# Other places, in the merged instruction order, for the three strands that run beside the cached pages

## The reference, cut to what matters

```python
# 1. the new tokens attend to the cached pages (64 pages of 128 tokens for each of 8 sequences)
kp = k_pool[page_table]; vp = v_pool[page_table]
s = concat([q @ kp, q @ k_new + mask]) ; w = softmax(s[0]) - lam * softmax(s[1]) ; o_b = w @ [vp, v_new]
# 2. gated delta rule over the prompt, 6 heads of 64: blocks with a triangular solve, then
v_new = u - w @ S ; o = q @ S + qk @ v_new ; S = S * g + k.T @ v_new
# 3. RWKV-7 over the prompt, 6 heads of 64, of the same shape, with its own decays, group norm and gate
# 4. keys and values of the prompt's memory (256 rows)
m = rmsnorm(mem, g) ; mk = m @ wk ; mv = m @ wv
```

## Time and profile before

| | |
|---|---|
| time, median of 3 runs | 5814.06 us (5811.03 to 5820.93) |
| the profiled execution | 5813.6 us, its span 5811.9 us |
| mean granted TensorE clock | 0.926 of full speed |
| busy, share of the span | PE 90%, PEld 56%, DVE 40%, ACT 26%, POOL 12% |
| the stage with the pages | from about 1351 to 2078 us of the span |
| that stage's PE | 555.3 us busy between 1353 and 2080 us |

### The profile page before, as it was taken

How to read it: one execution, slowest core, us unless ns; L and a number is a source line. 1 busy time by engine, 2 the same in 40 slices (tenths; PEclk the granted TensorE clock), 3 DMA queues, 4 the chain that set the end, 5 groups by cost and what they waited for, 6 DMA issues and landing times.

```text
span 5811.9 us, 91907 instructions
## 1 busy us (share of the span) xinstructions
PE 5255.0 (90%) x35274; PEld 3277.1 (56%) x35274; DVE 2329.3 (40%) x5433; ACT 1498.6 (26%) x3423; POOL 717.5 (12%) x935
## 2 busy tenths in 40 slices
PE   8989899996788667899989999999999899988998
PEld 5644445554556455666656555565555655656454
DVE  1156665553445423453434433343433534221322
ACT  3234543332222201221222221222212222112112
POOL 0012221111323201100101101011001110000000
PEclk9989999998989767799998999999999899997999
DMA  3110111104878523022231222312223122241232
GB/s 99 48 31 31 33 34 35 35 31 147 246 229 252 147 40 94 25 84 74 83 88 46 78 76 84 98 46 80 76 84 105 35 84 75 73 135 55 81 89 72
DMA packets 747337, 487.66 MB, mean 84 GB/s; under 512 B 78191, under 2 KB 728431, under 8 KB 746868
## 3 DMA queue, kind: packets, MB, share of 16 engines
q1 hardware_dynamic: 674134, 384.95, 23.2%
q10 hardware_dynamic: 60480, 63.27, 3.4%
q0 software_dynamic: 12288, 33.57, 1.9%
HBM read 432.57 MB, written 49.09 MB: 83 GB/s over the span
## 4 chain that ended last, share of the span: by engine, by line
PE 54%; DVE 4%; ACT 1%; issue 1%; DMA 1%; POOL 1%; SPq 0%; DVEq 0%; ACTq 0%; POOLq 0%
PE s_f_b L3493 27%; PE s_f_b L3551 11%; PE s_f_b L3542 2%; PE s_bank L2523 2%; PE s_bank L2530 2%; PE s_bank L2529 1%; DVE s_r_o L2795 1%; PE s_f_b L3532 1%; PE s_f_b L3498 1%; PE s_f_b L3514 0%; PE s_bank L2711 0%; PE s_bank L2666 0%; PE s_bank L3873 0%; PE s_bank L2708 0%; PE s_bank L3104 0%
## 5 line engine op out<-in xcount | busy, mean ns | idle before, releaser
L3493 PE MATMUL s_f_b<-s_f_h,s_f_W 128*128 128x416 f32 (+2 forms) x4480 | 1648.5, 523 | 26.3 <-DMA s_f_h<-o_t 17.1
L3493 PEld LDWEIGHTS s_f_b<-s_f_h,s_f_W 128*128 128x128 f32 x4480 | 845.2, 193 | 704.8 <-issue 585.8
L3551 PE MATMUL s_f_b<-s_f_a,s_f_W 128*128 128x416 f32 (+2 forms) x1760 | 640.0, 520 | 0.1
L539 PE MATMUL s_p_acc<-s_hT,s_p_W 128*128 128x416 f32 x1600 | 625.4, 538 | 6.8 <-DMA s_p_W<-in_w_in_dram 6.8
L3551 PEld LDWEIGHTS s_f_b<-s_f_a,s_f_W 128*128 128x128 f32 x1760 | 330.8, 191 | 266.2 <-issue 221.4
L539 PEld LDWEIGHTS s_p_acc<-s_hT,s_p_W 128*128 128x128 f32 x1600 | 299.4, 196 | 285.8 <-issue 269.3
L3751 DVE TENSOR_TENSOR s_f_xT<-s_f_xT,s_f_b 128x416 f32<-128x416 f32 (+2 forms) x160 | 93.7, 587 | 596.3 <-PE s_f_b L3551 531.4
L928 ACT ACTIVATE s_prob<-s_s_ps,s_ntop 128x512 f32<-128x512 f32 (+3 forms) x320 | 196.7, 620 | 369.1 <-DVE s_ntop L979 368.9
L3772 POOL TENSOR_TENSOR s_f_ex<-s_f_ex,s_f_mix 128x416 f32<-128x416 f32 (+2 forms) x105 | 112.2, 1069 | 1363.5 <-ACT s_f_mix L3580 1363.0
L3623 ACT ACTIVATE s_f_raw<-s_f_b 128x416 f32<-128x416 f32 (+2 forms) x110 | 56.9, 518 | 771.5 <-PE s_f_b L3493 771.5
L976 DVE TENSOR_REDUCE s_ntop<-s_s_ps 128x2 f32<-128x1024 f32 (+3 forms) x160 | 169.9, 1062 | 64.2 <-PE s_s_ps L876 61.7
(11 more groups left out here) (787 smaller groups left out, 7905.9 us busy)
## 6 DMA issues: line engine op xcount, KB each, us to landing
s_f_W<-in_ffn_w_in_dram SPq DMA_DIRECT2D x220, 512.0 KB, 3.8
s_K<-in_cache_diff_k_dram SPq DMA_DIRECT2D x384, 128.0 KB, 3.3
s_f_W<-in_ffn_w_out_dram SPq DMA_DIRECT2D x80, 448.0 KB, 3.8
s_V<-in_cache_diff_v_dram POOLq DMA_DIRECT2D x256, 128.0 KB, 3.8
s_V<-in_cache_diff_v_dram ACTq DMA_DIRECT2D x192, 128.0 KB, 3.7
cols_t<-s_p_out ACTq DMA_DIRECT2D x100, 208.0 KB, 1.9
s_f_W<-in_w_out_dram SPq DMA_DIRECT2D x40, 512.0 KB, 4.6
s_f_W<-in_ffn_w_out_dram SPq DMA_DIRECT2D x40, 512.0 KB, 4.1
```

The costliest lines, as they stand in the source:

```text
L539: mm = pe.matmul(self.acc[n % 2][:, 0:CH], self.W[:, u, k, :], self.hT[:, k, c * CH:(c + 1) * CH], start=(k == 0), stop=(k == KD - 1))
L3493: mm = pe.matmul(bank(u)[:, 0:G], w[:, k, :], h[:, k, 0:G], start=(k == 0), stop=(k == KD - 1 and kind != "op"))
L3551: mm = pe.matmul(bank(u)[:, 0:G], w[:, k, :], a[:, f % NA, 0:G], start=(k == 0), stop=(k == len(part) - 1))
```

## The change

`weave` gives way to `merge`, which takes an explicit list of places. The pages and the small loads keep theirs. The three strands beside the pages get new ones: D_ is spread evenly over 0 to 0.35, R_ over 0.37 to 0.72, W_'s first six slots stand at 0.735, 0.74, 0.775, 0.78, 0.785 and 0.79, and its `kv` slots at 0.81 to 0.89 in steps of 0.01. (`merge` stood in the kernel already, for a later stage.)

```diff
-                    n_slots = D_.slots + R_.slots + W_.slots
                     last = ((R_.stored, 16 * LEAD),)
+                    even = lambda lane: [(n + 0.5) / lane.slots for n in range(lane.slots)]
+                    stretch = lambda lane, a, b: [a + (b - a) * at for at in even(lane)]
+                    turn_at = stretch(D_, 0.0, 0.35) + stretch(R_, 0.37, 0.72) + [0.735, 0.74, 0.775, 0.78, 0.785, 0.79] + [0.81 + 0.01 * n for n in range(W_.slots - 6)]
                     turns = lambda eng, one, two, three: (
-                        in_turn(eng, in_turn(eng, one(eng), done, two(eng)), last, three(eng)), n_slots)
+                        in_turn(eng, in_turn(eng, one(eng), done, two(eng)), last, three(eng)), turn_at)
...
-                            weave((K_.sp(sp), K_.slots), turns(sp, D_.sp, R_.sp, W_.sp), (states(sp), len(loads)))
+                            merge((K_.sp(sp), even(K_)), turns(sp, D_.sp, R_.sp, W_.sp),
+                                  (states(sp), [(n + 0.5) / len(loads) for n in range(len(loads))]))
...
-                            weave((K_.pe(pe), K_.slots), turns(pe, D_.pe, R_.pe, W_.pe))
+                            merge((K_.pe(pe), even(K_)), turns(pe, D_.pe, R_.pe, W_.pe))
```

More of the change, by code:

```diff
@@ L4237, in _ @@
                             act.preload_act_table_set("natural_log_exp_and_others")
-                            weave((K_.act(act), K_.slots), turns(act, D_.act, R_.act, W_.act))
+                            merge((K_.act(act), even(K_)), turns(act, D_.act, R_.act, W_.act))
                         @block.vector
                         def _(dve):
-                            weave((K_.dve(dve), K_.slots), turns(dve, D_.dve, R_.dve, W_.dve))
+                            merge((K_.dve(dve), even(K_)), turns(dve, D_.dve, R_.dve, W_.dve))
                         @block.gpsimd
                         def _(pool):
-                            weave((K_.pool(pool), K_.slots), turns(pool, D_.pool, R_.pool, W_.pool))
+                            merge((K_.pool(pool), even(K_)), turns(pool, D_.pool, R_.pool, W_.pool))
                 levels = ss.sb("levels", [P, 7, P])
```

## The result

| | before | after |
|---|---|---|
| median | 5816.55 us (5 runs, 5811.03 to 5820.93) | 5844.84 us (5 runs, 5841.38 to 5847.66) |
| profiled span | 5811.9 us | 5846.0 us |
| granted clock, whole span | 0.926 | 0.924 |
| last store of the stage | 2076.11 us | 2111.64 us |

The ratio is 1.0049, with an interval of 1.0038 to 1.0059: the kernel became slower by half a per cent. The forecast was 5816 in a range of 5786 to 5843, so it missed on the slow side, where the chain rival stood (5838 to 5850). The stage's last store comes 35.5 us later and the span is 34.1 us longer, so all of the difference was made in this one stage.

The account below looks back on a forecast made before the run. PE was taken as the bound, near nine tenths busy nearly everywhere. K128 at 1949.1 - 14 + 26 + 4 + 43 + 7 + 7 - 9 + 3 = 2016, plus 63, gave 2079 for 2076.1, so 5816 us (5786 to 5843).

Parts of the forecast that it names:

- chain rival: Stage with cached pages: the recurrences' chain bounds, not PE; step 3 is 65 to 77 us, 5838 to 5850; chance 0.18.
- step 3: Ahead of K128, 32 pairs of strand slots without a page slot between: +43 us priced by hops, bounds 12 and 77.
- step 7: Ahead of K128, lower granted clock behind each of the new 7.5 us waits: +3 us.
- step 2: R_'s work and `tp` moved ahead of K128: +26 us of PE work, +4 of ordinary small waits.
- faster rival: Same stage: the pairs' hops vanish in waits the pages have anyway; 5786 to 5796 us; chance 0.28.
- post back: These slots side by side five times in D_ and R_: 18 us, the R_ tiles waiting 7.5 us each.
- mid flip: These slots side by side, among seven other pairs of step 3 at about 1 us each, 7 together.
- step 6: Waits for `E` and for the store at the change from D_ to R_ get hidden: -9 us (0 to -15).
- step 1: Stage's start: D_'s first load ahead of the pages brings K7 at 1398 for 1407: -14 us (9 to 19.5).
- steps 4 and 5: W_'s norm takes ACT from the pages, +7 us (2 to 12); lone page slots wait for V pages, +7 (0 to 15).
- DMA rival: V pages can't keep up in K115 to K127: 20 us and not 7, 5829; chance 0.10.
- Tail: From K128 to the stage's last store: 63 us, for 127 before.

Follow-up runs that it names:

- e5: The change with D_ spread evenly over 0 to 0.395, R_ over 0.395 to 0.80, and W_ later; ratio 0.9977 against the kernel before (-13 us).
- e10: The change with seven slots (back of D_1, D_2 and all R_ tiles, flip of R_1, R_2) put behind the next page slot; 1.0017 against the kernel before.
- e11: The change with D_ to 0.385, R_'s first slot at 0.387, its others evenly 0.395 to 0.803, W_ later; 0.9958 against the kernel before.
- e1: The kernel before with only D_'s first slot put ahead of the pages' first; ratio 1.0001 against the kernel before (+1 us).
- e12: e11 with the lane of small loads (constants and old states) starting at 0.1 of the order, not 0; ratio 0.9964 against the kernel before.
- e2: The change with W_ put back to its old places behind the pages; ratio 1.0088 against the kernel before (+51 us).
- e7: The change with D_ still dense (0 to 0.35), R_ widened to 0.37 to 0.80, W_ as in e5; ratio 1.0004 against the kernel before.
- e9: The change with D_ over 0 to 0.44, R_ still dense (0.45 to 0.80), W_ as in e5; ratio 1.0014 against the kernel before.

## Why the prediction was wrong, step by step

**The steps that failed are step 3, in the choice between its two bounds, and step 7, the clock.** Step 3 priced the pairs by the hop between two slots that stood uncovered at the end of R_ (43 us in all) and set aside "if the chain bound everywhere" (77). Step 7 gave the slower matmuls 3 us. The two traces say how far each was off. Up to the transposes of K127 (columns as in rows 2, before and after):

```profile
1351.00:1949.10 598.10, 461.96 (x5579) 328.58 (x5579) 281.75 (x600) 161.48 (x304) 171.68 (x277) 0.86 0.75 226
1351.00:2050.80 699.80, 513.15 (x6126) 370.68 (x6127) 301.65 (x641) 171.80 (x326) 178.63 (x288) 0.83 0.66 199
```

| up to K127, us | forecast | measured |
|---|---|---|
| start and key pages | -14 | -9 |
| waits of the recurrences (`s_shared`) | +47 (steps 2 and 3) | +76 |
| the pages' other waits | +5 (steps 4 to 6) | -17 |
| PE busy | +29 (26 of step 2, 3 of step 7) | +51 |
| in all | +67 | +102 (the parts, rounded, 101) |

The three rows of waits are sums over PE's list of waits, and the first has the idle time from 1351 us to PE's first product too. So the recurrences waited as the chain rival had it. The faster rival was right too, in that the pages' waits get shorter, but by 17 us only, and 6.9 of these stand before R_'s first product now. And 22 us of the 35 that are missing are PE's busy time: the work moved ahead was priced at 26 us, the rest is matmuls that took longer, at a granted clock of 0.83 for 0.86 on this path. In e5, with 18 pairs for 34, the whole loss is gone. Point by point:

- `post back`: the three R_ tiles waited 7.8, 8.3 and 8.9 us where 7.5 each was forecast. The mechanism and the size of the wait were right. Ahead of K127 only 3.2 us had stood before, so it is +21.7 there where step 3 put +14, having taken 5.6 off for waits in the page work. What became of those is part of the pages' row above.
- `mid flip`: put down at "about 1 each" among the seven other pairs. Before L2625 PE waited 8.5 and 10.3 us in the two tiles where the pair stands, for at most 4.4 before: +10 in all. The earlier trace rows had the warning, since 10.8 us were already waited for there in three waits, with a page slot between; I read it as a row of small waits and not as a chain with no slack left. That a hop is the price holds only where the strand had slack.
- D_'s `post back`: L3109 waited 9.5 us where some 4 was forecast for it; e10 takes it back to 0.4.
- *`Y` to `W`* (step 3, nine hops of 0.6): L2529 waited 10.2 us for R_'s copy on ACT, four times and up to 4.5 at a time. e10 still has these 10.2 us, e5 and e11 do not (1.6 and 0.6).
- *What is hidden* (step 6, -9): L1254 waited 18.2 us for 19.0, so the cover for `E` brought next to nothing. L1256's 9.4 us went, 6.9 of them at the change from D_ to R_, but R_'s first load, which step 6 named as not hidden, took their place: 9.2 us at L2609, for 1.8 before.
- *Start* (step 1, -14): PE's first L3025 came at 1360.71, in the forecast's 1358 to 1366, and K7 at 1396.4 for 1398. But K8 came at 1405.65, behind 6.33 us of waiting for key pages behind the 17 small loads: only 3.6 us earlier than before, with some three more D_ slots done. e1 (+1 us) and e12 show that the rest would not have lasted either.
- *Lone page slots and W_'s norm* (steps 4 and 5): K115 to K127 took 60.2 us where I had counted about 48, with 19.5 us idle, and ACT waited 7.66 us for W_'s rows where 6.5 was forecast. The 47 us of e2 put the lone slots where they were forecast, and 12 us on W_ beside them, for the 9 of its norm and transposes. No wait at L1567 is left (10.8 before). The DMA rival's sign, a wait over 5 us before L1274, did not come: 5.0 was the longest.
- *Clock* (step 7, +3): the wrong size. In the whole stage PE was busy 555.3 and 570.9 us with the same 6639 matmuls, so 15.5 of the 35.5 us are the same work done slower, at a granted clock of 0.84 for 0.86; and this is net of the tail, which ran at 1.00. e10 has 559.2 us of it. The low clock isn't only behind the five long waits: the fifth window has 0.83 over 337 us. What sets it was not found: e7, with less idle time than e9, has 12.7 us more of matmul time.
- *Tail*: 63 us forecast, 59.4 measured (61 from the start of K127's transposes), PE 95% busy. Right.

The lone slots ran at 232 GB/s, below the 293 of the earlier trace rows. The 358 GB/s of the Trainium skill ("DMA: Bandwidth & Descriptors", Specifications) is reached in no row here either, and changes nothing in the sum. For the clock, the window at 0.50 with which the stage begins agrees with the Trainium skill ("TensorE: Matmul & The Clock Gate", What's actually happening) in that half clock is where an idle PE stands.

The parts of the table are read from one trace each, and waits overlap in what they cause, so each is good to a few us only. What the runs measured is e10 (19 us for seven slots), e2 (23 us for W_'s places) and e5 (42 us for wider stretches, with W_ later). The mechanism of `post back` and `mid flip` is shown by e10; that the slower matmuls come with the dense order is seen, but the way by which they do stays open.

## What to carry to other kernels

Before strands are pressed together, look for the slots whose chain on another engine is longer than the work laid over it: a wait that is there already, with cover, says that the slack is zero and that each covering slot taken out costs its whole work. Then look at the busy time too: here 15.5 of the 35.5 us were the same matmuls at a lower granted clock. Spread the strands as wide as the tail allows and keep the covering slots between the first and last link of the long chains (`OD` to `back`, `proj` to `flip`, a load and its first use); seven slots put back behind one page slot gave 19 us here, and even steps ending at 0.80 in place of 0.72, with R_'s first load set ahead, made the same idea 24 us faster than the kernel before. A tail that gets 67 us shorter is no gain until the front has been counted, and a start that comes 11 us earlier isn't one until the end has.

## What was not expected of the hardware

The same 6639 matmuls took PE 553.6 us in e11, 555.3 before, and 570.9 in the change; 570.4 in e7, whose time is nearly that of before. In the change, the score products of the whole stage:

```profile
L1223 PE MATMUL s_s_ps<-s_kT,s_qd 128*32 128x512 f32 x512 | 68.5, 657 | 0.0
```

The mean is 657 ns for 632 in the earlier trace rows, although no wait stands before any of them. So work that doesn't itself wait gets slower too when the order changes. And more waiting doesn't mean a lower clock: e7 waited 165 us in 735 and e9 180 in 738, yet e7's matmuls took 12.7 us longer, and their granted clocks were 0.84 and 0.85. It isn't one odd execution: the mean granted clock of the whole kernel was 0.923 to 0.926 in e7's 11 runs and 0.926 to 0.928 in e5's 9. What makes the one worse than the other was not tried.
